# Woven attention of a decoder step on Trainium2: SyncE does a weight unit's loads and stores at the next unit's place in the order

## What is computed

```python
u = rmsnorm(h, attn_pre_g)
qa, kv_a, qi, ki, wi, qb, kv_b, g_a, g_b = project_inputs(u, w_in, pos)
o_a = dsa_attend(...)     # attention A: softmax over the top 256 keys of an indexer's score
o_b = diff_attend(...)    # attention B: (softmax(q1 k1) - lam * softmax(q2 k2)) v, then rmsnorm
merged = sigmoid(g_a) * (o_a @ w_br_a) + sigmoid(g_b) * (o_b @ w_br_b)
h = h + rmsnorm(merged @ w_out, attn_post_g)
gate, up = split(rmsnorm(h, ffn_pre_g) @ w_gate_up)
h = h + rmsnorm((silu(gate) * up) @ w_down, ffn_post_g)
h = h + sigmoid(h @ w_ple_gate) * (p @ w_ple_proj)
```

## Time and profile before

| | us |
|---|---|
| median of 3 runs (3669.53 to 3682.44) | 3674.64 |
| the profiled execution | 3671.66 |
| its span, first to last instruction | 3670.1 |
| PE busy (81% of the span) | 2985.0 |
| DVE busy (42%) | 1547.9 |
| ACT busy (16%) | 587.1 |
| POOL busy (16%) | 589.5 |
| mean granted TensorE clock | 0.894 |
| moved by DMA, mean of the span | 667.90 MB, 182 GB/s |

### The profile page before, as it was taken

The page is one execution under the profiler, slowest core; times in us unless marked ns, Lnnn a source line. Parts: engine busy times, 40 slices in busy tenths (PEclk is TensorE's granted clock), DMA queues, the critical chain, the costliest instruction groups (busy, mean ns, idle before and its releaser), DMA issues. The chain is left out here.

```text
span 3670.1 us, 69563 instructions
## 1 busy us (share of the span) xinstructions
PE 2985.0 (81%) x26553; PEld 2081.3 (57%) x26553; DVE 1547.9 (42%) x3004; ACT 587.1 (16%) x1294; POOL 589.5 (16%) x1089
## 2 busy tenths in 40 slices
PE   8999899548959688647698988888778989878697
PEld 4444366336749588644465655555545555545596
DVE  2222389837743677543643332253444333102211
ACT  1111210026634200000110110010111010101101
POOL 0000000000002000000023333333342334341000
PEclk9999699859979899878799998988988999889898
DMA  5232312140027344356789998999887989664695
GB/s 193 85 99 81 105 58 77 55 130 1 1 62 231 95 132 133 106 162 188 215 267 303 296 285 267 290 305 295 278 288 230 305 267 302 186 205 123 160 264 153
DMA packets 734994, 667.90 MB, mean 182 GB/s; under 512 B 69850, under 2 KB 607610, under 8 KB 734555
## 3 DMA queue, kind: packets, MB, share of 16 engines
q1 hardware_dynamic: 672730, 479.06, 43.7%
q0 software_dynamic: 61952, 184.62, 15.0%
HBM read 616.52 MB, written 46.98 MB: 181 GB/s over the span
## 5 line engine op out<-in xcount | busy, mean ns | idle before, releaser
L975 PE MATMUL sa_t<-tw_z,tw_w 128*128 128x352 f32 x1664 | 546.4, 484 | 19.0 <-DVE tw_x L1069 10.1
L1808 DVE STREAM_TRANSPOSE sa_key_b<-sa_ring_k 128x2048 f32<-128x2048 f32 x128 | 294.3, 2306 | 456.4 <-PE sa_s L1647 244.7
L1573 POOL DMA_DIRECT2D sa_ring_v<-cache_b_kv x512 | 275.6, 538 | 1097.2 <-PE sa_o L1714 738.6
L975 PEld LDWEIGHTS sa_t<-tw_z,tw_w 128*128 128x128 f32 x1664 | 323.7, 199 | 213.0 <-issue 55.6
L975 PE MATMUL sa_t<-tw_x,tw_w 128*128 128x352 f32 x960 | 310.4, 483 | 53.1 <-DMA tw_w<-w_br_a 45.7
L213 PE MATMUL pr_acc<-pr_w,pr_u_t 128*128 128x512 f32 (+1 forms) x864 | 326.6, 539 | 0.0
L1574 POOL DMA_DIRECT2D sa_ring_va<-cache_a_kv x512 | 275.0, 537 | 53.7 <-issue 24.9
L975 PEld LDWEIGHTS sa_t<-tw_x,tw_w 128*128 128x128 f32 x960 | 188.6, 200 | 163.5 <-issue 68.6
L213 PEld LDWEIGHTS pr_acc<-pr_w,pr_u_t 128*128 128x128 f32 x864 | 152.2, 190 | 167.9 <-issue 167.9
L1647 PE MATMUL sa_s<-sa_key_b,sa_q_pad 32*32 32x256 f32 x8192 | 195.7, 423 | 45.1 <-DVE sa_key_b L1808 41.3
L439 PE MATMUL sel_g<-sel_u,sel_gw 128*128 128x352 f32 x768 | 228.8, 461 | 0.0
(11 more groups left out here) (358 smaller groups left out, 3673.2 us busy)
## 6 DMA issues: line engine op xcount, KB each, us to landing
sa_ring_k<-cache_b_kv SPq DMA_DIRECT2D x512, 256.0 KB
sa_ring_v<-cache_b_kv POOLq DMA_DIRECT2D x512, 256.0 KB, 6.0
tw_w<-w_gate_up SPq DMA_DIRECT2D x88, 512.0 KB, 8.3
sa_ring_ka<-cache_a_kv SPq DMA_DIRECT2D x512, 64.0 KB
sa_ring_va<-cache_a_kv POOLq DMA_DIRECT2D x512, 64.0 KB, 5.6
tx_w<-w_gate_up SPq DMA_DIRECT2D x44, 512.0 KB
tp_w<-w_gate_up SPq DMA_DIRECT2D x44, 512.0 KB, 4.9
tw_w<-w_down SPq DMA_DIRECT2D x32, 512.0 KB, 6.4
```

Of the source, the lines that this page charges most:

```text
L975: ins = pe.matmul(bank[:, 0:self.width], self.w[:, at % self.SLOTS, k - lo, :], moving[:, k, :], start=(k == 0), stop=(k == kc - 1))
L1573: pool.dma_start(ring_v[:, n % RING, :], rows_of(cache_b, page, 1)).then_inc(v_in[n // 4 % 2], 16)
L1808: nc.vector.transpose(key_b[:, at:at + 4].rearrange("p g n s -> p (g n s)"), ring_k[:, at:at + 4, :].rearrange("p g e -> p (g e)")).then_i ...
```

## The change

In `sample_attend`, SP walks the held-back order that ACT and DVE walk already:

```diff
             load_sel(0)
-            for slot in order:
+            for slot in rest.late(order):
                 if slot[0] == "keys" and slot[1] + 1 < CHUNKS:
                     load_keys(slot[1] + 1, slot[2])
                 if slot[0] == "evacuate" and slot[1] + 1 < 2 * NB:
```

## The result

| | before | after |
|---|---|---|
| median of 4 runs | 3672.09 us | 3785.89 us |
| lowest, highest | 3669.37, 3682.44 | 3781.20, 3792.16 |
| ratio, 95% interval | | 1.0301 (1.0276 to 1.0326) |
| span of the profiled execution | 3670.1 | 3790.5 |

The medians lie 113.8 us apart, the two profiled executions 120.5. The execution that was profiled after the change, 3792.16 us, is the longest of its four; 6.6 us of its surplus lie in the last stage, which the change doesn't touch (249.9 us before, 256.5 after, from the first weight load to the end).

A forecast was written before the change was run, and what follows sets the result against it. PE, working in list order, was taken to bound the kernel, any wait adding time. Terms 95.2 + 19.6 + 5 + 4 - 10 = 113.8 us on 3671.66 gave 3785.5; 8 out of 10 lie from 3725 to 3840.

The forecast's parts named there:

- The main term: First piece, steps 25 to 33: seven down projection units wait for refills issued behind key loads, 95.2 us in sum.
- the landing: Time from issue to arrival of a down projection load behind keys: 8.3 us, the median for w_gate_up.
- The clock: PE runs at a slow clock after each new gap: 2.8 us for each of seven, 19.6, between 10 and 25.
- Gate, up and wo at nothing: Refills of gate, up and wo units leave later, but the three units in between cover them: no cost.
- one sign of being wrong: Listed as showing the forecast wrong: PE waits in gate and up units as well.
- Small units: Four-chunk ma and mb units at the start of each piece stall: 5 us in the first, 4 in the second.
- Keys earlier: Key loads that pass unit refills leave earlier: a gain of 10 us, from nothing to some 38.
- rival (a): Faster: earlier keys free PE and weights still come in time, minus 10 to 38 us, 3634 to 3662; chance 5%.
- Rival (c): Short landing, 3.97 us as in the tail, and key waits fully gained: 56 us, about 3728; chance 11%.
- rival (d): Long landing near 16.2 us as key, value and weight loads bunch up: about 3852 at its end; chance 11%.
- The sign: Whole kernel: slower given 0.92, same 0.03, faster 0.05.

The follow-up runs named there:

- e6_big_only: Against the kernel before, only wo, gg and up units are held back in SP's order: 3665.84 us, 0.9975 times.
- half-key pair: Two kernels loading half of each branch B key row, one in the changed kernel's SP order, one in the old: 3724.16 against 3626.35 us.

## Why the prediction was right

**The main term** was the right mechanism at the right size: 95.2 us in seven gaps, measured 95.3. The single terms were off in both directions, and that the sums agree to 0.1 us is luck:

| | dn1 | dn2 | dn3 | dn4 | dn5 | dn6 | dn7 |
|---|---|---|---|---|---|---|---|
| predicted | 13.9 | 16.1 | 14.8 | 5.5 | 12.4 | 13.0 | 19.5 |
| measured gap | 12.0 | 14.2 | 17.5 | 5.1 | 15.4 | 15.5 | 15.6 |
| issue of the first load to PE's resuming | 6.4 | 6.6 | 8.6 | 11.6 | 9.7 | 8.8 | 5.3 |

The last row is the landing that I had taken as 8.3 for all. Its mean is 8.1, so the choice of `w_gate_up`'s row over `w_down`'s was right: by 6.4 the sum would have been 13 us short. It ranges from 5.3 to 11.6. Added over the seven gaps, the refills left 74.8 us behind the starts of their units, where 70.7 were worked out; the landings took 57.1 us in place of 58.1; and the first 16 matmuls took 36.5 us in place of 33.6. The first two make the gaps 4.1 us longer and 1.0 shorter, the third 2.9 shorter, and they cancel. `dn7` shows it most: four key groups stand before its refill, but it landed in 5.3 us, so its gap was 3.9 us shorter than forecast. That the medians are 113.8 us apart, the forecast to the digit, is a coincidence too: the profiled executions are 120.5 apart.

At that place the fit of the Trainium skill (DMA: Bandwidth & Descriptors, section Anatomy of one DMA), made for software-issued DMAs, gave an estimate of 3.2 us for 512 KB. The seven landings were 5.3 to 11.6 us, and the measurement decides; they were issued by SP, three at a time, behind eight pages of keys.

Of the last stage the prediction says that nothing competes there and that PE waits 3.97 us for a load. The row is the load's whole time from issue to landing; PE's own wait before it was 2.2 us, and the DMA engines were busy 61% from 3560 to 3640 us. As a landing time, which is how the sum uses it, 3.97 stands.

**The clock** was given 19.6 us. The 28 matmuls behind a gap would take 28/44 of 13.28, 8.45 us; they took 10.24, 10.09, 10.56, 11.17, 11.00, 11.48, and for `dn7` 10.95, in sum 16.3 us more. The clock fell with the gaps. The stretch of `dn3`'s gap shows a mean granted clock of 0.65, between the levels of 0.5 and 1.0 (columns as in the earlier trace rows, the granted clock third from the end):

```profile
2325.00:2345.00 20.00, 2.49 (x8) 1.36 (x7) 4.08 (x4) 0.00 (x0) 2.43 (x5) 0.65 0.96 270
```

By this count the term was 3 us too large; I had taken it from `dn0`, which stands behind two waits, 6.37 and 2.86 us. Counted over all of PE's work between the scores of chunks 25 and 33, busy time grew from 161.7 to 181.2 us, 19.5, which is the term. PE's idle time there grew from 27.7 to 116.9 us: the seven waits brought 95.3, and other short ones, that had been there before, fell by 6.1. Together 19.5 + 89.2 = 108.7 us, the 108.8 of the table.

**Gate, up and wo at nothing**: right. Two waits of 1.2 and 1.3 us are all that the changed kernel's timeline shows, and `e6_big_only` has one of 0.8 and no cost. Taken by the letter, one sign of being wrong, that PE waits in `gg` and `up` units as well, did appear, with 1.3 us in 88 such units. The largest landing of a `w_gate_up` load rose from 16.2 to 18.6 us, more than the least cover of 12.9 us that the prediction found, but long landing and little cover seldom met.

**Small units**: 5 us at the start of the first piece. Chunk 0's scores were 4.4 us later, but 1.0 of it was there when the stage began; PE's wait for `mb5` was 3.36 where it had waited 0.71 for `ma6`. In the second piece I took 4; PE's waits for these loads there went from 10.5 to 10.1 us, but chunk 41 is 5.5 us later than chunk 38, and 3 of it are made good by chunk 63. The split wasn't measured further.

**Keys earlier** at 10 us: key waits fell by 9.1 us, and 8 us is what `e6_big_only` gained alone. The rival (a), that 490.9 and 211.5 us of waiting stand for a gain, is refuted by the same run. The three small terms together, 5 + 4 - 10, make -1 us; outside steps 25 to 33 the changed kernel lost 4.9, of which 1.0 was there before the stage. So this part was some 5 us off, and which of the three it was stays open.

**Rival (c)**, short landing, and **rival (d)**, long landing, ask for the same mechanism with another size; 8.1 us decided between them. In (d) the Trainium skill's rule that each DMA engine takes turns between queues (DMA: Bandwidth & Descriptors, section Queues, rings and completion order) would have halved the rate of the refills. The half-key pair shows 13.5 us of the waits for 0.4 of the key bytes, not the bulk of the loss; how much of that is queues taking turns no run here separates.

**The sign** rested on one comparison, and it can be carried over: the last key load is issued after the unit's start in all seven steps, and in six of them by 8 to 15 us, where the unit needs its second load after 4.8. There no landing, however fast, could have made it good.

## What to carry to other kernels

When work is moved along an in-order queue, list what it now stands behind and what that waits for: here the refill came to stand behind loads that can't leave before the very step that needs the refill. A ring's reach must be counted in the largest unit's loads, not in units: beyond the unit at work, four slots hold three more units of one kind and one third of a unit of another. Giving slots back load by load, in the old order, was worth 40 us at no cost in memory. An issuing engine's waiting is no cost in itself, and a row of it that shrinks may only have moved: 138 us less waiting for units came with 110 us more for transposes, and the two were worth 8 us of time.

## What the runs showed of the hardware

One 512 KB load, issued with two others, took 3.97 us to land in the last stage, and the first of three took 5.3 to 11.6 us behind 2.6 MB of keys and beside the values. SP needs about 1.3 us for each page of keys, a register load and two DMAs of 0.33 us each, so eight pages hold it for 10.4 to 11.5 us in the first two gaps, with 128 KB pages as with 256 KB ones. Three weight loads issued right behind eight pages occupied SP for 4.0 to 7.1 us in the first six gaps (6.63 at 2335.54), in place of 1.6, and with half keys for 1.8 to 4.8 us. So issuing itself gets slower with more bytes ahead in the queue, which I had not counted; it didn't enter the gaps, since PE waits for the first of the three.
